# Second table loaded a whole chunk at a time, with the weights rounded between a chunk's two high parts

## What is computed

```python
def peer_ffn(xn, wq, keys, u_tab, v_tab):
    q = (xf @ wq).reshape(t, PEER_HEADS, 2, PEER_HALF)
    ...
    eidx = jnp.take_along_axis(cidx, pos, axis=-1)
    gate = jax.nn.softmax(top, axis=-1).astype(xn.dtype)
    ...
        u = jnp.take(u_tab, ib, axis=0)
        act = jax.nn.gelu(jnp.einsum("thkd,td->thk", u, xb), approximate=False)
        v = jnp.take(v_tab, ib, axis=0)
        return jnp.einsum("thk,thkd->td", gb * act, v)
```

## Time and profile before

| | us |
|---|---|
| median of 3 runs | 1820.53 |
| lowest and highest | 1818.84, 1822.06 |
| profiled execution, its time | 1824.04 |
| its span, in which all rows below lie | 1822.2 |
| PE busy | 1768.0 (97%) |
| DVE busy | 1273.4 (70%) |
| ACT busy | 863.4 (47%) |
| POOL busy | 504.9 (28%) |

### The profile page before, as it was taken

The page is one execution under the profiler, slowest core; times in us unless marked ns, Lnnn a source line. Parts: engine busy times, 40 slices in busy tenths (PEclk is TensorE's granted clock), DMA queues, the critical chain, the costliest instruction groups (busy, mean ns, idle before and its releaser), DMA issues.

```text
span 1822.2 us, 32600 instructions
## 1 busy us (share of the span) xinstructions
PE 1768.0 (97%) x12247; PEld 1603.5 (88%) x12247; DVE 1273.4 (70%) x2054; ACT 863.4 (47%) x1434; POOL 504.9 (28%) x336
## 2 busy tenths in 40 slices
PE   7999969999999999999999999999999999999998
PEld 7998969999999999999999999977767777777775
DVE  7787676666989989444444555557887888888885
ACT  6544744343443444444444333355455455545554
POOL 0000000000006877777872000056831111111100
PEclk9999989999999999999999999999999999999999
DMA  7654528787557778777776887898999999999983
GB/s 241 204 196 138 179 74 249 227 248 235 187 182 194 185 187 190 188 187 188 190 190 194 253 257 252 269 338 305 336 350 338 341 351 345 338 351 338 340 313 112
DMA packets 186533, 445.61 MB, mean 245 GB/s; under 512 B 59360, under 2 KB 94448, under 8 KB 177904
## 3 DMA queue, kind: packets, MB, share of 16 engines
q1 hardware_dynamic: 146976, 373.47, 61.3%
q0 software_dynamic: 39504, 71.55, 15.1%
HBM read 423.79 MB, written 20.57 MB: 244 GB/s over the span
## 4 chain that ended last, share of the span: by engine, by line
PE 68%; DMA 14%; DVE 9%; ACT 4%; issue 4%; ACTq 0%; DVEq 0%; SPq 0%
PE ps L1452 19%; PE ps L1454 19%; PE ps L1453 19%; DMA raw<-v_tab 13%; DVE low L829 4%; ACT high L558 3%; PE ps L1681 2%; PE ps L1697 2%; PE ps L1683 2%; PE ps L1695 2%; PE ps L1693 2%; DVE big L1377 2%; DVE big L839 0%; PE ps L1646 0%; DVE big L1155 0%
## 5 line engine op out<-in xcount | busy, mean ns | idle before, releaser
L829 DVE TENSOR_TENSOR low<-raw,high 128x1024 fp32r<-128x1024 f32 x638 | 767.0, 1222 | 430.3 <-ACT high L558 385.5
L1452 PE MATMUL ps<-act_hi,high 128*128 128x256 f32 x3056 | 872.6, 286 | 24.8 <-DVE act_lo L862 13.1
L1453 PE MATMUL ps<-act_lo,high 128*128 128x256 f32 x3056 | 867.7, 284 | 0.0
L1454 PE MATMUL ps<-act_hi,low 128*128 128x256 f32 x3056 | 867.6, 284 | 0.0
L558 ACT ACTIVATE high<-raw 128x1024 fp32r<-128x1024 f32 x638 | 657.0, 1058 | 338.0 <-DMA raw<-v_tab 206.7
L1452 PEld LDWEIGHTS ps<-act_hi,high 128*128 128x128 f32 x3056 | 589.6, 193 | 28.8 <-issue 17.1
L1453 PEld LDWEIGHTS ps<-act_lo,high 128*128 128x128 f32 x3056 | 589.7, 193 | 0.1
L1454 PEld LDWEIGHTS ps<-act_hi,low 128*128 128x128 f32 x3056 | 589.6, 193 | 0.0
L750 ACT ACTIVATE big<-ps 128x192 f32<-128x192 f32 x128 | 42.4, 331 | 424.7 <-PE ps L1454 393.9
L519 POOL DMA_INDIRECT big<-v_tab,half_sb x64 | 86.2, 1346 | 566.2 <-DVE big L1377 355.0
L499 POOL DMA_INDIRECT gate_scratch<-gates_sb,cells_sb x128 | 214.1, 1672 | 65.8 <-issue 65.8
(11 more groups left out here) (214 smaller groups left out, 1477.2 us busy)
## 6 DMA issues: line engine op xcount, KB each, us to landing
raw<-u_tab SPq DMA_DIRECT2D x256, 512.0 KB
raw<-v_tab SPq DMA_DIRECT2D x256, 512.0 KB
raw<-w_in SPq DMA_DIRECT2D x62, 512.0 KB
raw<-w_out SPq DMA_DIRECT2D x32, 512.0 KB
raw<-w_q SPq DMA_DIRECT2D x32, 512.0 KB
gate_scratch<-side SPq DMA_DIRECT2D x32, 384.0 KB, 6.1
big<-gate_scratch SPq DMA_DIRECT2D x16, 768.0 KB, 7.5
act_scratch<-side SPq DMA_DIRECT2D x32, 128.0 KB
```

Of the source, the lines that this page charges most:

```text
L829: V.tensor_tensor(slot(low, s), slot(raw, s), slot(high, s).bitcast(F32), ALU.subtract).then_inc(lo_done, 1)
L1452: mm(acc, wh, a_hi, start=(kk == 0), stop=False)
L1453: mm(acc, wh, a_lo, start=False, stop=False)
L1454: ins = mm(acc, wl, a_hi, start=False, stop=(kk == KT - 1))
```

## The change

The second table's chunks are loaded by `load_rows`: one transfer of 2048 columns (8 KB a partition) for both slots of a pair, issued when both low parts of the chunk two before are done. It counts on the semaphore of the pair's first slot; ACT waits for it at high part 0 and not again at high part 1 (`landed=True`). In the steps of this stage ACT rounds the weights between the two high parts, and DVE makes the weights' low part between the two low parts. The first table and all other weights are loaded as before.

```diff
+            def load_rows(e):
+
+                c, s = C_V_TAB + e, 2 * ((C_V_TAB + e) % 2)
+                sp.wait_ge(lo_done, 2 * c - 2)
+                sp.dma_start(raw[:, s * PIECE:(s + 2) * PIECE], v_tab[e]).then_inc(raw_in[s], 16)
+
             for e in range(2):
-                load(C_V_TAB + e, (C_V_TAB + e) % 2, v_tab[e])
+                load_rows(e)
             save_act(N_KEYS // EXPORT - 2)
-            load(C_V_TAB + 2, C_V_TAB % 2, v_tab[2])
+            load_rows(2)
...
             for e in range(3, N_KEYS):
-                load(C_V_TAB + e, (C_V_TAB + e) % 2, v_tab[e])
+                load_rows(e)
...
-            def cut_high_piece(c, par, half):
+            def cut_high_piece(c, par, half, landed=False):
                 s = 2 * par + half
-                act.wait_ge(raw_in[s], 16 * ((c - par) // 2 + 1) if isinstance(c, int) else 8 * (c - par) + 16)
+                if not landed:
+                    act.wait_ge(raw_in[s], 16 * ((c - par) // 2 + 1) if isinstance(c, int) else 8 * (c - par) + 16)
...
-            def expert_step(e):
+            def expert_step(e, whole=False):
 
                 c, par = C_U + e, (C_U + e) % 2
-                cut_high(c + 1, 1 - par)
+                for half in range(2):
+                    cut_high_piece(c + 1, 1 - par, half, landed=whole and half == 1)
...
-            expert_step(N_KEYS - 1)
+            expert_step(N_KEYS - 1, whole=True)
 
             def v_step(e, par):
 
-                cut_high(C_V_TAB + e, par)
+                cut_high_piece(C_V_TAB + e, par, 0)
                 round_w(e, par)
+                cut_high_piece(C_V_TAB + e, par, 1, landed=True)
...
                 par = (C_V_TAB + e) % 2
-                cut_low(C_V_TAB + e, par)
+                cut_low_piece(C_V_TAB + e, par, 0)
                 weights(e, par)
+                cut_low_piece(C_V_TAB + e, par, 1)
```

## The result

| | us |
|---|---|
| before, median of 4 runs | 1819.77 (1818.84 to 1822.06) |
| changed, median of 4 runs | 1836.49 (1834.47 to 1837.94) |
| ratio, with its 95% interval | 1.0089 (1.0072 to 1.0107) |
| changed, profiled execution and its span | 1837.25, 1835.4 |

The change costs 16.7 us. The direction is the one that was forecast, the size is not: 40 us were forecast. The measured time lies inside the stated range of 1806 to 1905 us. The spans of the profiled executions differ by 13.2 us (1835.4 and 1822.2); that of the kernel before was some 4 us slower than its median.

A forecast was written before the change was run, and what follows sets the result against it. PE was taken as the bound, the raw ring just hidden behind it. (6.4 + 3.9) / 2 = 5.15 us a chunk, 0.36 more, x 111 chunks = +40 us, other terms 0: 1860 us median; range 1806 to 1905.

The forecast's parts named there:

- What bounds the kernel: Second-table stage: PE at 4.79 us a chunk, 4% from its own 4.60, with the buffer ring just hidden behind it.
- the ring: Raw's two chunk places: twice a chunk's time is issue to landing plus landing to free, or 9.2 us if PE is slower.
- Part 1: Second table's chunk in one transfer: the whole chunk's raw is free 3.88 us after landing; a lone piece at least 2.46.
- Part 2: Weights between the two parts: PE starts 1.24 us earlier after a landing; up to 0.19 us a chunk, or 0.
- L of a 1 MB load: Issue to landing of a second-table chunk beside gathers: taken as 6.4 us, between 4.0 and 8.8.
- The removed issues: 128 of 256 load issues on SP go away; worth 0, as SP isn't short of time.
- The term of nothing for 8 KB rows: DMA engines move 8 KB rows no cheaper than 4 KB ones, 328 ns against twice 161; no gain counted.
- slower: Chance that the changed kernel is slower by over 0.2% (3.6 us): 0.68.
- The rule of the Trainium skill: DMAs of at least 1 MiB; its fit gives 4.4 us a chunk load, ring 8.3 us, PE the bound.
- Faster: Rival: gathers fall between loads if their phase holds; stage gains 0.09 to 0.19 us a chunk, 1800 to 1811; chance 0.22.
- Same: Rival: DMA bytes are the bound at 340 GB/s; both kernels run at 4.8 us a chunk, 1817 to 1824; chance 0.10.
- Much slower: Last rival: each gather falls in full on a load; up to 5.9 us a chunk, 1943; decides above 1905; chance 0.12.

The follow-up runs named there:

- the run with two transfers: Changed kernel with its waits, but each chunk loaded by two 512 KB transfers issued back to back; 1875.3 us, and 1867.4 us when repeated.

## Why the prediction was right or wrong

**What bounds the kernel**: right, and now shown. Twice the time of a chunk is issue to landing plus landing to free, unless PE is slower; a third place in the ring brings PE's pace at once, and so does taking the gathers away. One reading was off: it took the least time from landing to free, 2.46 us, for that of a piece, and so 7.1 us for its landing. By the landing events of the kernel before, a piece is free 3.0 to 3.2 us after it has landed, and lands in 6.4 to 6.6.

**Part 1, the time from landing to free**: 3.88 us worked out, 3.87 in an undisturbed turn, about 4.2 on average, because a sparse unit is sometimes in the way on DVE. That waiting was left out of the sum, which makes it 0.15 us a chunk too small.

**Part 2, the weights between**: right in sign. It was worth 0 in the forecast and 0.4% alone; in the ring of whole chunks its worth is under what the times can tell.

**L of a 1 MB load is the step that failed.** The forecast took 6.4 us, the middle of 4.0 and 8.8, and the trace has 5.6: 0.4 us a chunk too much, times 111 is 44 us. With the missing 0.15 (17 us) the sum would have been (5.6 + 4.2) / 2 = 4.9 us. The bounds held both. What was wrong in the argument was how it went from pieces to a chunk: its upper limit was 7.1 us for a piece plus 1.3 for more bytes, where a piece took 6.5, and pieces of 5.95 and 6.06 us were taken to say that 5 is too little beside gathers. In the changed kernel a 1 MB load takes 4.85 us when few gather packets are beside it and 6.75 with a whole gather, and the first kind is common enough that the average is 5.6, under that of today's pieces of half the size. Why whole chunks land sooner than pieces in this ring is not shown. The row is not the reason (one transfer in 4 KB rows has 5.66 on average); with two transfers at the same waits it is 5.96 from the second issue, or 6.33 from the first.

That the run with two transfers comes near the forecast (5.2 us a chunk and 1867 to 1875 us, against 5.15 and 1860) is a coincidence: its parts are 5.96 us to landing and 4.45 from landing to free, not 6.4 and 3.9. The removed issues were booked at 0, and no run here shows another value against the kernel before, which issues each piece when its own place is free. Only against two transfers issued together does the single one save 0.37 us of issue in every turn. The term of nothing for 8 KB rows was right (410 and 410).

Two slips moved nothing: h_back and g_last are loaded beside six chunks, not five, and the chance of "slower" should be 0.66 and that of "same" 0.12 if 0.02 of the forecast's and the last rival's chances are not clearly slower.

**The rule of the Trainium skill**, larger DMAs (DMA: Bandwidth & Descriptors, section Bandwidth). The fit stands in that page's section Anatomy of one DMA — SWDGE (gpsimd) path, and is for transfers that POOL issues; these loads are issued by SP. Its estimate for a load alone, 4.4 us, is near the 4.7 us of the run without gathers, and the rule's direction, fewer and larger transfers, agrees with the runs at equal waits (1837 against 1867 us). The conclusion that the ring would turn at PE's pace did not come true, as gathers add 0.9 us to 4.7.

**The rivals.** Faster fell, but its mechanism is partly there: 41 of the 103 loads took under 5 us, mostly with little of a gather beside them, but 38 took over 6, and the phase does not hold by itself. Same, with the bytes as the bound, fell with the three places at 355 to 361 GB/s. Much slower fell: even two transfers stay at 5.2 us.

**What was to be seen**: the count per 100 us is 80 to 84 where 75 to 80 was said; GB/s 327 to 344, not 310 to 325; ACT's wait is well over 206.7 (294.5) and PE's waits over 60 (68.0), as said.

## What to carry to other kernels

A ring of buffers has a turn, from issue to landing and from landing to free; divided by the number of places, it is the time of one chunk. Before changing the size of its transfers, compare that turn with the pace of the engine it feeds; here only 5% were between them, a unit that may be used only whole cost more than the saved transfers gave back, and one more place was worth more than either. At equal waits one transfer was better than two issued back to back, since the second issue is in the turn.

## What was not expected of the hardware

- One 1 MB transfer against two of 512 KB issued together: 0.3 us a chunk less, but only while gathers run; 0.37 us a turn of it is the second issue. Rows of 8 KB against rows of 4 KB inside one transfer: no difference in time (410 and 410).
- The engine time a MB of a queue is no fixed price: the same 1 MB loads have 42.1 us beside gathers and 45.4 without them.
- Without gathers a 1 MB load lands in 4.7 us and a 512 KB piece, with nearly two of them under way at once, in 4.3. With a whole gather beside it a 1 MB load takes 6.75 us on average.
- A program can stand nearly still for some 50 us, with DMA at 0 to 42 GB/s and the granted clock at 0.50, the lower of its two levels, while POOL goes on with cell gathers. This was seen in the trace of one program, whose other three executions took as long; no other trace has more than a small dip there.
